# SyncE waits for the first half of the first weight tile before it asks for the second half

## What is computed

```python
h = _rms(x, g_mix[l])
z = h @ w_in[l]
za, zu, zv, zq, zg = jnp.split(z, SPLITS, axis=-1)
ya = jax.nn.gelu(_s5(za, ...))            # diagonal state space model
yb = _sgu(zu, zv, ...) @ w_b_out[l]       # gated MLP over blocks of tokens
yc = _mem_xattn(zq, mem, g_mem[l], w_kv[l]) @ w_c_out[l]
merged = gates[:, :, 0] * ya + gates[:, :, 1] * yb + gates[:, :, 2] * yc
x = x + merged @ w_out[l]
hf = _rms(x, g_ffn[l])
x = x + (jax.nn.silu(hf @ w_gate[l]) * (hf @ w_up[l])) @ w_down[l]
```

## Time and profile before

| | before |
|---|---|
| median of three runs | 784.72 us (784.19 to 785.12) |
| the profiled execution, its own time | 784.56 us |
| its span in the profile | 782.7 us |
| TensorE busy | 765.4 us (98%) |
| VectorE busy | 541.1 us (69%) |
| ScalarE busy | 379.6 us (49%) |
| GpSimd busy | 317.3 us (41%) |
| moved by DMA | 121.97 MB, 156 GB/s on average |
| granted TensorE clock | 0.998 |

### The profile page before, as it was taken

How to read it: one execution, slowest core, us unless ns; L and a number is a source line. 1 busy time by engine, 2 the same in 40 slices (tenths; PEclk the granted TensorE clock), 3 DMA queues, 4 the chain that set the end, 5 groups by cost and what they waited for, 6 DMA issues and landing times.

```text
span 782.7 us, 9799 instructions
## 1 busy us (share of the span) xinstructions
PE 765.4 (98%) x3584; PEld 631.4 (81%) x3584; DVE 541.1 (69%) x726; ACT 379.6 (49%) x546; POOL 317.3 (41%) x163
## 2 busy tenths in 40 slices
PE   8999999999999999999999999999999999899996
PEld 7778787788888888887788788888888888678885
DVE  6999996684848484345765777777777787336675
ACT  6895467644545434543434344444434333334463
POOL 4456565233333333444444343444444444730000
PEclk9999999999999999999999999999999999999999
DMA  8733423032222442232334465666665667767743
GB/s 274 288 144 108 135 81 108 28 95 94 74 89 81 128 141 82 83 106 89 98 94 147 141 210 179 212 228 207 219 197 191 208 199 252 209 217 244 271 162 121
DMA packets 39666, 121.97 MB, mean 156 GB/s; under 512 B 4048, under 2 KB 4176, under 8 KB 37840
## 3 DMA queue, kind: packets, MB, share of 16 engines
q1 hardware_dynamic: 39632, 121.52, 46.8%
HBM read 104.99 MB, written 16.52 MB: 155 GB/s over the span
## 4 chain that ended last, share of the span: by engine, by line
PE 73%; DVE 14%; ACT 3%; issue 3%; POOL 3%; DMA 2%; SPq 0%; ACTq 0%; DVEq 0%; POOLq 0%
PE bank L1514 20%; PE bank L1516 20%; PE bank L1515 20%; PE bank L1882 3%; PE bank L1884 3%; PE bank L1883 3%; DVE pow_tmp L944 2%; DVE s5p L944 2%; POOL w_lo L493 2%; DVE tab_tmp L944 1%; DMA raw<-mix_dram 1%; POOL w_lo L539 1%; PE bank L1754 1%; DMA xT<-xt_dram 1%; DVE parts L944 1%
## 5 line engine op out<-in xcount | busy, mean ns | idle before, releaser
L493 POOL TENSOR_TENSOR w_lo<-raw,w_hi 128x1024 fp32r<-128x1024 f32 x90 | 218.0, 2422 | 300.9 <-ACT w_hi L550 300.9
L550 ACT ACTIVATE w_hi<-raw 128x1024 fp32r<-128x1024 f32 x112 | 118.6, 1060 | 278.2 <-PE bank L1516 264.6
L1514 PE MATMUL bank<-h_hi,w_hi 128*128 128x512 f32 x608 | 238.5, 392 | 1.6 <-issue 0.8
L1516 PE MATMUL bank<-h_hi,w_lo 128*128 128x512 f32 x608 | 236.7, 389 | 0.0
L1515 PE MATMUL bank<-h_lo,w_hi 128*128 128x512 f32 x608 | 236.6, 389 | 0.0
L1514 PEld LDWEIGHTS bank<-h_hi,w_hi 128*128 128x128 f32 x608 | 114.1, 188 | 27.6 <-issue 2.8
L1516 PEld LDWEIGHTS bank<-h_hi,w_lo 128*128 128x128 f32 x608 | 114.1, 188 | 23.8
L1515 PEld LDWEIGHTS bank<-h_lo,w_hi 128*128 128x128 f32 x608 | 114.2, 188 | 23.5 <-issue 0.2
L498 POOL TENSOR_TENSOR w_lo<-raw,w_hi 128x512 fp32r<-128x512 f32 x48 | 68.9, 1457 | 57.1 <-ACT w_hi L550 50.7
L944 DVE TENSOR_TENSOR lo<-raw,hi 128x1536 fp32r<-128x1536 f32 (+1 forms) x19 | 35.3, 1856 | 43.6 <-ACT hi L860 43.6
L944 DVE TENSOR_TENSOR mix<-mix 128x512 f32<-128x512 f32 x44 | 47.3, 1075 | 12.0 <-DMA mix<-w_dram 10.8
(11 more groups left out here) (288 smaller groups left out, 1400.2 us busy)
## 6 DMA issues: line engine op xcount, KB each, us to landing
raw<-w_dram SPq DMA_DIRECT2D x112, 512.0 KB, 3.4
mix<-w_dram SPq DMA_DIRECT2D x11, 1024.0 KB, 7.8
mix_dram<-mix SPq DMA_DIRECT2D x11, 1024.0 KB, 6.3
raw<-w_dram SPq DMA_DIRECT2D x34, 256.0 KB, 4.1
raw<-mix_dram SPq DMA_DIRECT2D x30, 256.0 KB, 3.7
half_dram<-odd SPq DMA_DIRECT2D x11, 256.0 KB, 8.0
second<-half_dram SPq DMA_DIRECT2D x3, 768.0 KB, 7.2
raw<-mix_dram SPq DMA_DIRECT2D x3, 768.0 KB, 4.3
```

The costliest lines, as they stand in the source:

```text
L493: nc.gpsimd.tensor_tensor(w_lo[:, s, :], raw[:, s, :], fv(w_hi[:, s, :]), ALU.subtract).then_inc(w_ready, 1)
L550: nc.scalar.activation(w_hi[:, slot, :], raw[:, slot, :], ACT.Copy).then_inc(w_rounded, 1)
L1514: mm(out, a[0], b[0], start=first, stop=False)
L1516: return mm(out, a[1], b[0], start=False, stop=last)
```

## The change

After w0a and x0 have been asked for, SyncE waits until w0a has landed in full (16 increments on `first_loaded[0]`). Then it asks for w0b and all that follows, in the order of before. The other engines' programs are the same.

```diff
@@ -362,6 +362,8 @@
 
             sp.dma_start(small[:, 0:C_BRE], small_d[:, 0:C_BRE]).then_inc(vec_loaded, 16)
             for k in range(4):
+                if k == 1:
+                    sp.wait_ge(first_loaded[0], 16)
                 load_first(k // 2, k % 2)
                 load_x(k)
             load_x(4)
```

## The result

The changed kernel takes 786.5 us (median of 8 runs, 785.59 to 787.85), the kernel before 784.73 in the same job (8 runs, 783.64 to 785.41). The ratio is 1.0025 with a 95% interval of 1.0016 to 1.0035: **slower by 1.8 us**, where I had forecast no change. The profiled execution took 785.82 us.

A forecast was written before the change was run, and what follows sets the result against it. Mostly TensorE's own work bounds the kernel; its start has two chains, TensorE's from x0 and VectorE's from x3. With -0.8 and -0.1 us, the later counting, the sum was 0.0: 784.7 us, range 783.4 to 786.4.

The forecast's parts named there:

- The wait itself: SyncE's queue at the start: w0b and six issues behind it go out 1.88 us later; tile 2 not delayed.
- x0 alone: Start: x0 lands at 4.7 to 6.4 without competition; TensorE's chain gains some 0.8 us, worthless unless VectorE's follows.
- the list of signs: Profile signs expected at the start, among them a TensorE wait at step 6 or earlier longer than 0.29 us.
- x3, which sets VectorE's chain: Last of the first eight loads: x3 lands at 11.3 against 11.46, 0.1 us earlier, taken as nothing.
- The sum: Whole kernel: VectorE's chain -0.1, TensorE's -0.8, the later counts, 0.0 after rounding; forecast 784.7 us.
- the slower one: First loads: the delay goes through, x3 lands 1.88 us late and the end is 786.6 us; chance 0.14.
- the 0.69 MB moved ahead of need: Bytes of x4 and tile 2 moved by 11.45, taken as showing that x3's bytes could come sooner.
- The faster rival: First loads: landings as early as the queue allows, ScalarE the bound, both chains 1.1 us earlier, 783.6 us; chance 0.22.
- Spread: VectorE's small steps beside GpSimd's w_lo: one collision more or less is 1.1 us, either way; range 783.4 to 786.4.

The follow-up runs named there:

- wait_idle: Kernel before with the same wait placed ahead of w1b, where w0a is due to land anyway: 785.06 us, ratio 1.0003.
- again: The changed kernel run once more, unaltered, for its scatter and a second profile: 786.29 us, ratio 1.0018.
- dve_late: Kernel before, loads untouched, with two unused VectorE products added ahead of its row of small steps: 786.89 us, ratio 1.0024.
- late_turn: Kernel before with four small s5p steps, the end of the third table step, moved behind the four uT products: 785.43 us, ratio 1.0003.
- dve_late_turn: dve_late with the four small s5p steps that end the third table step moved behind the uT products: 786.48 us, ratio 1.0018.
- filler: Changed kernel with the first 512 KB of the tokens asked for between x0 and the wait: 787.34 us, ratio 1.0027.
- x_contig_changed: Changed kernel with the transposed input laid out so that each eighth is one contiguous DRAM block: 785.47 us, ratio 1.0004 to the kernel before.

## Why the prediction was wrong

**The wait itself**: right. w0b at 3.99 (4.06 said), tile 2 not delayed by the queue (8.88), a wait as such free (`wait_idle`).

**x0 alone**: the number came, but not for the reason given, and of no use, as said. x0 is rounded at 4.62, the first product starts at 6.63 (5.92 in `again`), and both executions end later. But x0 is rounded at 4.92 to 5.05 in three of the five profiles with the old loads too, where w0b and x1 are asked for as early as ever (`dve_late`, `late_turn`, `dve_late_turn`), and the first product starts at 6.16 to 6.81 there. The 6.40 of the kernel before belongs to its one profile. An earlier TensorE chain with a later VectorE chain is a longer wait, 1.75 us at step 5; this too was on the list of signs.

**x3, which sets VectorE's chain**: this is the step that failed. I took the four and a half microseconds from w0b to x3 of the kernel before as the time of the backlog of bytes, and so as the same behind any start: 6.86 + 4.46 = 11.3. Measured are 12.19 - 6.86 = 5.33, and 13.05 - 6.98 = 6.07 in `again`. In the other two profiles of the changed loads it is 6.03 and 5.18. With the old loads it is 4.30 to 4.73 in four profiles, and 5.57 in the one where w0b came early, at 5.93; x3 is at 11.45 to 11.59 in all five. The bytes moved ahead of need before the change were not a mere queue in front of x3; the rate behind the wait is lower (233 GB/s against 378), and neither the idle hole (`filler`) nor the layout alone (`x_contig_changed`) explains it. Why the first loads run so slowly behind the wait stays open. My bounds for x3, 10.2 to 13.3, held both values; the value taken was at the wrong end.

By the rule of the Trainium skill that the prediction set beside this step ("DMA: Bandwidth & Descriptors", section "Anatomy of one DMA"), w0b would be rounded at 6.7 and x3 at 9.7, an estimate: the first agrees with 6.86, the second doesn't agree with 12.19. The section gives its 2.0 us and 436 GB/s for DMAs that GpSimd issues, and these are issued by SyncE, so no run here tests the rule on its own ground.

**The sum**: "the later of the two counts" was right, `dve_late` shows it from the other side. But the size at the end was off as well: x3 0.7 to 1.6 us late gave 1.5 to 1.8 in the medians, and `dve_late` gave 1.77 for a row 1.1 late. I had priced each 0.1 at 0.1. The sum had no term for TensorE's clock. Two things are seen beyond it in profiles, a last stretch of the row that meets a `w_lo` (`dve_late`), and TensorE's clock after its wait (`again`); taking either away moved the median by less than the intervals can show. By the mean clocks of the runs the second would be 1.9 us in seven of twenty.

**The rivals**: the slower one was the case, in its mechanism (the delay goes through VectorE's row) and close to its number, 786.6 against 786.5. It was right by a mixture of two errors: it asked for x3 1.88 us late, which is too much, and left out what comes on top. Against it I had put "the 0.69 MB moved ahead of need", the same argument that failed above, and so gave it 0.14. The faster rival is refuted by ScalarE's four waits for DMAs.

**Spread**: the measured median is 0.1 us above my range. The first three runs of the kernel before span 0.9 us; the 35 runs of a later job span 783.23 to 789.0. A collision more or less was counted once; the changed kernel has one more in four steps (3.85 us instead of 1.78) and is spared others, since its `xdiag` is only 0.47 late where `h_lo` of the eighth 5 was 2.8 late.

## What to carry to other kernels

A load asked for ahead of need is not only a crowd before the urgent one: it starts the stream, and a pause in the queue was paid here by the last of the eight loads, not by those next to it. Before ordering a start anew, find which landing the end answers to (here x3, the last, through a row of small steps on another engine), and treat a gain for the first load as worth nothing. When latency must be carried over to another issue order, take the range between "the spacing stays" and "the delay goes through" as equally likely, unless a row tells them apart.

## What was unexpected of the hardware

- The rate of the first loads depends on more than how many are outstanding: 233 to 278 GB/s from 7 to 11 us behind the wait (four executions), 255 with the hole before it filled, 310 with each part of the input side by side in DRAM, 357 to 378 in five executions without the wait.
- A small VectorE step of 128x16 takes 1.26 us beside a `w_lo` of GpSimd instead of 0.17, seven times as long. So two tenths of a microsecond of shift can change a row by microseconds, in both directions.
- TensorE's granted clock was 0.50 (1.2 GHz) soon after waits of 2.16, 2.23 and 1.79 us, and stayed at 1.00 after waits of 2.00, 1.79 and 1.75 in other executions. Near 675 us TensorE waits 2.9 us for a `w_lo` in the kernel before and in the changed one; the clock fell behind it in the second alone. In `again` the fall went with about 1.4 us of lost time.
- The same kernel rounds x3 at 12.19 in one execution and at 13.05 in another, and x0 scatters by 1.5 us with the old loads, so one profile's milestones are good to about a microsecond, and small differences of medians need a dozen runs.
